# A hybrid retention/HGRN layer: eight level products in one run, and the retention scores one chunk boundary later

## What is computed

```python
proj = h @ w_in                                   # 2048 x 9216
rq, rk, rv, rg, hq, hf_f, hf_b, hi, hg = jnp.split(proj, 9, axis=-1)
# retention: decay depends on the distance alone
scores = jnp.einsum('bhid,bhjd->bhij', qc, kc) * intra
# HGRN: every key channel d has its own decay, b = cumsum(log f)
diff = b[:, :, :, None, :] - b[:, :, None, :, :]
decay = jnp.exp(jnp.where(causal, diff, -jnp.inf))
scores = jnp.einsum('bhid,bhjd,bhijd->bhij', qc, kc, decay)
o = (jnp.einsum('bhij,bhjv->bhiv', scores, vc)
     + jnp.einsum('bhid,bhdv->bhiv', qc * jnp.exp(b), s))
...
out = jnp.concatenate([o_r, o_h], axis=-1) @ w_out
x = x + gate[:, None, :] * out
```

## Time and profile before

| | |
|---|---|
| median of 3 runs | 1402.61 us (1402.18 to 1403.21) |
| the profiled execution | 1402.38 us, span 1400.6 us |
| busy: PE | 1383.8 us, 99% |
| DVE | 999.3 us, 71% |
| ACT | 483.7 us, 35% |
| POOL | 368.1 us, 26% |
| chain that ended last | PE 95%, DMA 3%, DVE 1% |

### The profile page before, as it was taken

How to read it: one execution, slowest core, us unless ns; L and a number is a source line. 1 busy time by engine, 2 the same in 40 slices (tenths; PEclk the granted TensorE clock), 3 DMA queues, 4 the chain that set the end, 5 groups by cost and what they waited for, 6 DMA issues and landing times.

```text
span 1400.6 us, 24702 instructions
## 1 busy us (share of the span) xinstructions
PE 1383.8 (99%) x10042; PEld 1165.8 (83%) x10042; DVE 999.3 (71%) x1330; ACT 483.7 (35%) x842; POOL 368.1 (26%) x292
## 2 busy tenths in 40 slices
PE   7999999999999999999999999999999999999997
PEld 5788898889888988898889888988898888888886
DVE  5555676667689889988898889877676768532345
ACT  4323243234333333342334333333333344221234
POOL 0000114311532153215321532153206225201220
PEclk9999999999999999999999999999999999999999
DMA  9994442435343535454444454433443357182235
GB/s 387 418 418 161 117 126 69 120 72 139 95 161 108 172 94 178 111 153 119 161 116 140 128 166 114 130 97 106 106 106 86 103 151 278 53 305 93 90 106 210
DMA packets 207735, 212.40 MB, mean 152 GB/s; under 512 B 144256, under 2 KB 156816, under 8 KB 202768
## 3 DMA queue, kind: packets, MB, share of 16 engines
q1 hardware_dynamic: 207600, 210.89, 47.9%
q10 hardware_dynamic: 32, 0.02, 0.0%
HBM read 182.27 MB, written 24.40 MB: 148 GB/s over the span
## 4 chain that ended last, share of the span: by engine, by line
PE 95%; DMA 3%; DVE 1%; SPq 0%; issue 0%; ACT 0%; DVEq 0%; ACTq 0%
PE ps L2122 10%; PE ps L2124 10%; PE ps L2123 10%; PE ps L1957 9%; PE ps L1958 8%; PE ps L1959 8%; PE ps L1933 8%; PE ps L2299 5%; PE ps L2301 5%; PE ps L2300 5%; DMA area<-in_w_mod 2%; PE ps L2139 2%; PE ps L1964 2%; PE ps L1965 2%; PE ps L1966 2%; PE ps L1923 2%
## 5 line engine op out<-in xcount | busy, mean ns | idle before, releaser
L1201 DVE TENSOR_TENSOR w_lo<-area,w_hi 128x1024 fp32r<-128x1024 f32 x143 | 190.3, 1331 | 206.7 <-ACT w_hi L729 206.7
L729 ACT ACTIVATE w_hi<-area 128x1024 fp32r<-128x1024 f32 x143 | 151.5, 1059 | 495.5 <-PE ps L2124 266.1
L2122 PE MATMUL ps<-w_hi,hT_hi 128*128 128x512 f32 x640 | 251.1, 392 | 0.0
L2124 PE MATMUL ps<-w_hi,hT_lo 128*128 128x512 f32 x640 | 249.1, 389 | 0.0
L2123 PE MATMUL ps<-w_lo,hT_hi 128*128 128x512 f32 x640 | 249.0, 389 | 0.0
L1957 PE MATMUL ps<-hT_hi,w_hi 128*128 128x512 f32 x512 | 204.8, 400 | 0.0
L1958 PE MATMUL ps<-hT_lo,w_hi 128*128 128x512 f32 x512 | 199.7, 390 | 0.0
L1959 PE MATMUL ps<-hT_hi,w_lo 128*128 128x512 f32 x512 | 199.6, 390 | 0.0
L2124 PEld LDWEIGHTS ps<-w_hi,hT_lo 128*128 128x128 f32 x640 | 120.1, 188 | 25.2
L2122 PEld LDWEIGHTS ps<-w_hi,hT_hi 128*128 128x128 f32 x640 | 120.2, 188 | 24.3
L2123 PEld LDWEIGHTS ps<-w_lo,hT_hi 128*128 128x128 f32 x640 | 120.2, 188 | 24.1
(11 more groups left out here) (282 smaller groups left out, 2427.7 us busy)
## 6 DMA issues: line engine op xcount, KB each, us to landing
area<-in_w_in SPq DMA_DIRECT2D x144, 512.0 KB, 4.2
area<-in_w_mod SPq DMA_DIRECT2D x26, 1024.0 KB, 12.3
area<-in_w_out SPq DMA_DIRECT2D x38, 512.0 KB, 3.9
gate_raw<-in_w_gate SPq DMA_DIRECT2D x32, 512.0 KB, 4.0
gate_raw<-in_w_mod SPq DMA_DIRECT2D x6, 1024.0 KB, 12.1
o_hi_scratch<-area SPq DMA_DIRECT2D x56, 80.0 KB, 2.4
o_lo_scratch<-area SPq DMA_DIRECT2D x56, 80.0 KB, 2.4
hT_hi<-o_hi_scratch SPq DMA_DIRECT2D x14, 320.0 KB, 7.0
```

What stands on the lines that cost most here:

```text
L729: act.activation(split_weights(h, n)[0], raw[:, n % 3, :], ACT.Copy).then_inc(wt_hi.sem, 1)
L1201: v.tensor_tensor(lo, raw[:, n % 3, :], hi.bitcast(F32), ALU.subtract).then_inc(wt_lo.sem, 1)
L2122: mm(out, hT_hi[:, k, tile_cols(t)], w_hi[:, n % 2, w], start=k == 0, stop=False)
L2124: i = mm(out, hT_lo[:, k, tile_cols(t)], w_hi[:, n % 2, w], start=False, stop=k == KT - 1)
```

## The change

Two moves.

- **Level products.** PE no longer has products behind chunks 3, 5, 7 and 9, but all eight behind chunk 8 (`SCORED`), in `all_scores`. Each level gets a buffer of its own (`decayed`), in areas whose other use is over until then; differences wait for the end of the burst behind chunk 1 (`pe_hu`) and no longer for products. `DIFFERENCES` and `DECAYS` say in which item a level is prepared, on DVE, POOL and ACT alike. Levels 2 to 6 write their scores packed, 32 columns per tile (`packed_tile_scores`), and `place_all` spreads them under the masks in DVE's item 9. The key sum is in POOL's item 7. `gate_reduced` is alone behind chunk 5.
- **Retention scores** of head h stand ahead of the retention updates, behind chunk 0 of head h+1, and their masks in DVE's items 0; only the last head keeps the old place. The loads of old states, the rope DMAs and a few waits follow the buffers.

The last head's own recurrence, behind the loop, keeps its form.

```diff
+DIFFERENCES = {3: (1,), 4: (2, 3), 5: (4, 5), 6: (6,)}
+DECAYS = {4: (1,), 5: (2, 3), 6: (4, 5), 7: (6,)}
+SCORED = 8
+PACKED, PACK = 2, TILES * QUAD
...
+        decayed = {0: XE[:, 0], 1: KL, 2: XE[:, 1], 3: halves(area[:, RET1:RET1 + 2 * T]),
+                   4: halves(area[:, KTL0:KTL0 + 2 * T]), 5: halves(area[:, KTL0 + 2 * T:KTL0 + 4 * T])}
...
-                if n == 6 and h is not None:
+                if n == 14 and h is not None:
...
             def differences(h, following, level):
...
-                if due(pe_level, h, level):
+                if following is not None and level:
+                    dve.wait_ge(pe_hu.sem, pe_hu.at(h))
+                elif due(pe_level, h, level):
                     dve.wait_ge(pe_level.sem, pe_level.at(h, level))
...
+            def place_all(h):
+                dve.wait_ge(pe_level.sem, pe_level.at(h))
+                v.tensor_copy(tiles(hsT[:, P:T]), tiles(ps[:, A, :])).then_inc(h_sT.sem, 1)
+                v.tensor_copy(hsT[:, 0:P], ps[:, DD, 0:P]).then_inc(h_sT.sem, 1)
...
+                for level in range(PACKED, LEVELS):
...
+                    v.copy_predicated(quads, where, scores).then_inc(h_sT.sem, 1)
...
                     if n == 0:
                         retention_silu(prev, 0)
-                        own_decay(prev, 0)
+                        own_decay(prev, h, 0)
+                        masked_latents(prev, A)
+                        masked_context(prev, ps[:, BB, P:2 * P])
...
-                    if n == 4:
-                        place(prev, h, 0)
-                    if n in (4, 6, 8):
-                        differences(prev, n - 3)
-                        differences(prev, n - 2)
-                    if n == 6:
-                        place(prev, h, n - 4)
-                    if n == 8 or n == 10:
-                        place(prev, h, n - 4)
-                        place(prev, h, n - 3)
-                    if 4 <= n < 3 + LEVELS:
-                        own_decay(prev, n - 3)
+                    for level in DIFFERENCES.get(n, ()):
+                        differences(prev, h, level)
+                    for level in DECAYS.get(n, ()):
+                        own_decay(prev, h, level)
+                    if n == SCORED + 1:
+                        place_all(prev)
...
+                    if n == SCORED - 1:
+                        pool.wait_ge(la.sem, la.at(prev, LEVELS))
+                        key_sum(prev, K[:, 0, :])
...
+            def packed_tile_scores(out, keys, queries):
+                for c_ in range(4):
+                    rows = slice(c_ * QUAD, (c_ + 1) * QUAD)
+                    i = mm(out[rows], keys[:, rows], queries[:, rows], start=True, stop=True)
+                return i
...
                     if n == 0:
+                        retention_scores(prev, A, ps[:, BB, P:2 * P])
                         retention_updates(prev)
...
-                    if n == 3:
-                        level_scores(prev, h, 0)
-                        level_scores(prev, h, 1)
-                    if n in (5, 7, 9):
-                        level_scores(prev, h, n - 3)
-                        if n == 5 and 0 <= gate_block(prev) < GATE_BLOCKS:
-                            gate_reduced(prev)
-                        level_scores(prev, h, n - 2)
+                    if n == 5 and 0 <= gate_block(prev) < GATE_BLOCKS:
+                        gate_reduced(prev)
+                    if n == SCORED:
+                        all_scores(prev, h)
```

More of the change, by code:

```diff
@@ L381, in out_bank, with ctx_scores, level_queries, level_keys @@
             return ((0, 1, 2, 3, BB), (A, C, DD, 0, 1))[nb % 2][t]
-        def ctx_scores(following, product):
+        def ctx_scores(product):
+            return ps[:, BB if product <= 2 else DD, 0:P]
+        def level_queries(following, level):
             if following is None:
[L386 to L391, removed]
+                return XE[:, level % 2, 0, :]
+            return decayed[level][:, 0, :] if level in decayed else sT
+        def level_keys(following, level):
+            if following is None:
+                return XE[:, level % 2, 1, :]
+            return decayed[level][:, 1, :] if level in decayed else kl_tokens[:, 8 * P - T:]
+        def packed_scores(level):
+            i = level - PACKED
+            return ps[:, C, i * PACK:(i + 1) * PACK] if i < 3 else ps[:, DD, P + (i - 3) * PACK:P + (i - 2) * PACK]
         def query_chunk(h):
@@ L959, in items @@
                     context_columns(h)
-                if prev is not None and n in (4, 6, 8):
-                    decays(prev, n - 3)
-                    decays(prev, n - 2)
+                if prev is not None:
+                    for level in DECAYS.get(n, ()):
+                        decays(prev, h, level)
                 if n == 11:
@@ L1032, in _ @@
             items(CHUNKS - 1, last, None)
-            decays(last, 0)
+            decays(last, None, 0)
             tokens_context(last)
@@ L1673, in _ @@
             hgrn_silu(last, 0)
-            place(last, None, 3)
-            differences(last, 4)
+            place(last, 3)
+            differences(last, None, 4)
             hgrn_silu(last, 1)
@@ L1691, in _ @@
             hgrn_silu(last, 3)
-            place(last, None, 7)
+            place(last, 7)
             hgrn_silu(last, 4)
@@ L1813, in key_factors, with differences @@
                 g.tensor_tensor(KL, KL, K, ALU.mult).then_inc(h_kl.sem, 1)
-            def differences(h, level):
+            def differences(h, following, level):
                 half = P >> (level + 1)
-                x = blocks(XE[:, level % 2, 1, :], level)
+                x = blocks(level_keys(following, level), level)
                 bf, bb = blocks(B[:, 0, :], level), blocks(B[:, 1, :], level)
@@ L1822, in differences @@
                 pool.wait_ge(h_scan.sem, h_scan.at(h))
-                if due(pe_level, h, level):
+                if following is not None and level:
+                    pool.wait_ge(pe_hu.sem, pe_hu.at(h))
+                elif due(pe_level, h, level):
                     pool.wait_ge(pe_level.sem, pe_level.at(h, level))
@@ L1885, in _ @@
             last = HEADS - 1
-            key_decay(last, 0)
+            key_sum(last, XE[:, 1, 1, :])
+            key_decay(last, None, 0)
             key_factors(last)
             for level in range(1, LEVELS):
-                differences(last, level)
-                key_decay(last, level)
+                differences(last, None, level)
+                key_decay(last, None, level)
             pool.wait_ge(fnw_in.sem, fnw_in.at(0))
```

277 lines of the change are left out of this document (154 added, 123 removed).

## The result

The changed kernel takes 1443.59 us in the median (1439.32 to 1444.17, 4 runs) against 1402.39 us (1402.15 to 1403.21): a ratio of 1.0287, 95% interval 1.0275 to 1.0300. That is 41 us slower, outside the range of the prediction and ten times the loss it gave. The profiled execution took 1444.17 us, 41.8 more than the profiled one of before.

The account below looks back on a forecast made before the run. PE's executed work between first and last head was taken as the time (95% of the chain). 1402.38 - 5.1 - 0.1 + 9.2 = 1406.4, as a median 1406.6 us; range 1397.0 to 1411.0.

Parts of the forecast that it names:

- Step 1, level products in one run: Merging PE's product bursts behind chunk 8 saves 0.90 us in three heads and 0.60 in four: 5.1 us gained.
- The clock rival: PE's clock drops in the longer uniform run of narrow matmuls, costing a few microseconds more; chance 0.02.
- Step 2, retention scores: Scores moved ahead of the retention updates join an existing burst, gaining 0.1 us; masks ready about 2.5 us early.
- Step 3, the wait for `w_lo` at chunk 7: PE waits 2.3 us for DVE's split at chunk 7 in four heads with closing gate steps: 9.2 us lost.
- The ledger: Step 3's sum of DVE and POOL work from closing gate steps to chunk 7's split, which ends at 520.67.
- No new wait: POOL lags by four operations or more, or DVE takes turns better; PE never waits: 1397.4 us, chance 0.19.
- A second wait at the run: PE waits behind chunk 8 for levels and key sum, 0.5 us in seven heads: 1410 us, chance 0.08.

Follow-up runs that it names:

- four and three bursts: Changed kernel's eight products split into four bursts behind chunks 5, 6, 7 and 8: 1402.03 us; or into three behind 5, 7 and 8: 1399.79 us.
- the ladder: Kernel before plus 20 to 160 constant 32x32 matmuls per head behind chunk 15, taking four row parts in turn: 1437.18 us rising over the heads, 1429.38 falling.
- the kernel with three bursts: Changed kernel with levels 0 and 1 behind chunk 5, 2 to 4 behind 7, 5, 6 and the diagonal behind 8: 1399.79 us.
- the run with the 50 records of 128-column weights: Changed kernel with one matmul of 128 rows replacing four of 32 rows per tile of levels 2 to 6, 340 instructions instead of 640: 1442.13 us.

## Why the prediction was wrong

**Step 1, level products in one run: failed.** It gave a gain of 5.1 us, and the chunks that it is about took 41.9 us more. "A burst has 0.30 us of its own, whatever it holds" was read from bursts of 80 and 40 records and carried on to 320; what it takes to supply PE with the instructions of such a run was put at nothing. The pace was right (12 ns a record until the stop), the start right (0.32 between four and three bursts, and the gate matmuls alone cost 0.8 us, where 0.7 was given), and the form cost nothing. What the step left out is that PE's instructions are data and come by DMA: 79 packets of 16 KB (1.29 MB) for the 20084 records of PE and PEld, some 254 in a piece. At the pace of the big matmuls a piece lasts some 29 us. In the run it lasts 1.5, and 640 instructions are two and a half pieces.

Counted over all runs: none of the 28 bursts of 160 instructions in the kernel before and none of the 35 of 240 stood still; of the 28 bursts of 320, eight did, in their second half or just behind; of the 14 of 640, all. A burst of 320 that stopped lost 1.9 to 4.2 us so, one of 640 between 4.0 and 5.3, and on top comes what the lowered clock costs.

The Trainium skill, Runtime: NRT & Kernel Launch, Instruction fetch mechanics, says that an engine fetches its next 16 KB page by its own queue while it executes the present one, and that this is mostly hidden because instructions are issued more slowly than pages come. The pieces and their size agree with the trace; the hiding doesn't hold for matmuls of 12 ns. It gives TensorE 2048 instructions of such memory and elsewhere only two pages; the runs fit the two, since a run of 640 first stopped after 308 to 528 of its instructions. I had the row on the page, and priced only what has a line of the kernel.

**The clock rival** had 0.02. It came, as a consequence: in all 14 runs of 640 instructions the granted clock fell to its lower level during a standstill or within 0.3 us of its end, while some shorter standstills (1.3 us at 100 matmuls of the ladder, 2.2 at 160) left it at 1.00. Not for the reason given there, though a row of 50 matmuls with 128 columns of weights and 32 moving ones did bring it without a standstill.

**Step 2, retention scores: right.** 1.1 us moved from one boundary to another, nothing gained or lost that could be measured; no wait for the masks.

**Step 3, the wait for `w_lo` at chunk 7: failed.** 9.2 us were given, 0 came. PE came to chunk 7 when it was forecast to (in head 3 2.1 us earlier than before, counted from chunk 2; 2.13 were given), but in the four heads the split was ready 2.0 us ahead of it in the changed kernel, and in the other heads, where the ledger has 3.4 us less to do, 0.8. The ledger let each of POOL's operations push one of DVE's. The prices are right where both run in turn (1.00 and 1.49 us, as in the earlier trace rows), but POOL's first key decay was held off for 4 us by DVE's unbroken row, so DVE did a split and six more operations free of charge, and the split for chunk 6 started on time. In head 3, nine of the ledger's sixteen POOL operations were over when the split for chunk 7 ended (527.75), and from the gate steps (509.20) to there DVE took 18.6 us instead of the 22.8 of the ledger: with its own 13.0 as given, POOL's part, with 0.5 us of waiting for ACT in it, was 5.6 and not 9.8. The Trainium skill, SBUF — State Buffer, Terms, has the shared port as a lock that one side holds while the other blocks. Here it was POOL that blocked, for longer than any one operation of DVE; that page's rule alone doesn't give it.

**The rivals.** "No new wait" is what happened to DVE and POOL, by its own condition (POOL lags by four operations or more), and its 1397.4 us would have been near: the kernel with three bursts, without standstills, is at 1399.8, and the ten burst starts that the full change saves on top, at 0.32 us, bring an estimate of 1396.6. "A second wait at the run" named the right place for a wrong reason. No case had a standstill without a semaphore, so the range could not hold it.

## What to carry to other kernels

Count the instructions of a stretch, not only its time: at 12 ns a record, 240 in a row never stopped PE here, 320 did or didn't by where a 16 KB border fell, and 640 cost 4 to 5 us and a lowered clock each time. So here merging bursts pays until the supply of instructions runs out: three bursts of two to three products beat both kernels, 1399.79 us. And when a wait has no releaser ("issue"), look for the instruction queue's packet in it before looking at the operands.

## What the runs showed of the hardware

- PE stopped in the middle of an accumulation for 3.10 us, where the program has no wait, and resumed behind one 16 KB packet of the instruction queue. From the packet's window in the run of head 1 of the changed kernel, where PE stood from 260.5 to 263.73:

```profile
DMA  0000090000000000000000000000000000000000
...
q8 instruction: 1, 0.02, 2.8%
```

  The packet starts 0.5 us into the standstill (it is in the sixth slice, and a slice is 0.08 us), lasts 2.8% of 16 engines' 3.23 us, that is 1.45 us, and PE goes on 1.3 us behind its end. What sets the moment at which it is asked for is open: in head 3 it came 2.2 us into the standstill, under heavy weight traffic, and here 0.5, under none. That traffic delays it was not tried.
- 32x32 float32 matmuls cost 12 ns a record when they take the four row parts in turn, and 32 when they stay in one. With 128 columns of weights and 32 moving ones a record took 115.
- With PE busy throughout, the granted clock fell to 0.50 between 4.5 and 7.1 us behind the start of the run with the 50 records of 128-column weights, in all seven heads, and it stayed at 1.00 in 9 us of 32x32 ones in one row part. Why the one and not the other stays open.
- A POOL operation that takes 0.86 us undisturbed took 5.21 beside a DVE that did not pause for the first 4.5 us of it, and DVE's took no longer; where both began together (in the trace before, DVE at 505.32 and POOL at 505.36), they went in turn from DVE's next operation on, at the price of the earlier trace rows. Which of the two ways it goes was not settled beyond this place.
